# Where V is turned and split in a stick-breaking attention block: whole on TensorE before it is stored, or chunk by chunk after it is loaded

## The reference, cut to what matters

```python
z = einsum('bhqd,bhnkd->bhqnk', q_blk, k_pre) * scale
log_1m = where(valid, log_sigmoid(-z), 0.0)
within = einsum('bhqnk,kj->bhqnj', log_1m, suffix)
w = where(valid, exp(log_sigmoid(z) + within + later[..., None]), 0.0)
o = einsum('bhqnk,bhnkd->bhqd', w, v_pre)
```

## Time and profile before

| | |
|---|---|
| median of three runs | 2293.88 us |
| the profiled execution | 2293.96 us |
| its span, first to last instruction | 2292.2 us |
| TensorE busy | 2279.5 us, 99% |
| VectorE, ScalarE, GpSimd busy | 1444.4, 1060.2, 1224.3 us |
| granted TensorE clock | 0.999 of full speed |

### The profile page before, as it was taken

One profiled execution on the slowest core, in us unless ns is written; L12 is line 12 of the kernel. 1 busy time (PEld: TensorE's weight loads), 2 busy tenths in 40 slices (PEclk: granted clock), 3 DMA queues, 4 the chain that ended last, 5 costly groups with the idle time before them and its releaser, 6 DMA issues.

```text
span 2292.2 us, 29991 instructions
## 1 busy us (share of the span) xinstructions
PE 2279.5 (99%) x10824; PEld 1886.8 (82%) x10824; DVE 1444.4 (63%) x1658; ACT 1060.2 (46%) x1627; POOL 1224.3 (53%) x847
## 2 busy tenths in 40 slices
PE   9999999999999999999999999999999999999998
PEld 6888888888878888888888888888888778888887
DVE  7565542764496478568877777733854585486476
ACT  5555542343385255332576676632342583355220
POOL 1666643865456355435476566644863556456341
PEclk9999999999999999999999999999999999999999
DMA  6544422123334345373344543322133334354442
GB/s 234 187 159 158 139 83 97 55 83 129 113 104 133 134 124 148 105 284 138 108 159 139 165 156 124 125 92 78 56 120 124 92 103 134 130 156 132 152 161 83
DMA packets 114419, 297.84 MB, mean 130 GB/s; under 512 B 11232, under 2 KB 41056, under 8 KB 113248
## 3 DMA queue, kind: packets, MB, share of 16 engines
q1 hardware_dynamic: 112544, 290.68, 38.6%
q10 hardware_dynamic: 1728, 5.24, 0.7%
HBM read 216.19 MB, written 71.30 MB: 125 GB/s over the span
## 4 chain that ended last, share of the span: by engine, by line
PE 97%; DVE 1%; DMA 1%; issue 0%; DVEq 0%
PE J L823 21%; PE J L825 21%; PE J L824 21%; PE ZZ L995 8%; PE AO L995 8%; PE ZZ L825 2%; PE ZZ L824 2%; PE ZZ L823 2%; PE AO L825 2%; PE AO L824 2%; PE AO L823 2%; PE AO L949 1%; PE JX L949 1%; PE ZZ L1030 1%; PE JX L825 1%; PE JX L823 1%
## 5 line engine op out<-in xcount | busy, mean ns | idle before, releaser
L2341 POOL TENSOR_TENSOR WLS<-SR,WHS 128x512 fp32r<-128x512 f32 x264 | 414.3, 1588 | 110.1 <-ACT WHS L1161 102.5
L823 PE MATMUL J<-XBH,WHS 128*128 128x512 f32 x1152 | 452.3, 393 | 0.0
L825 PE MATMUL J<-XBH,WLS 128*128 128x512 f32 x1152 | 449.1, 390 | 0.0
L824 PE MATMUL J<-XBL,WHS 128*128 128x512 f32 x1152 | 448.9, 390 | 0.0
L823 PE MATMUL J<-XBH,WH 128*128 128x512 f32 x864 | 340.3, 394 | 0.4 <-DVE WL L1764 0.2
L825 PE MATMUL J<-XBH,WL 128*128 128x512 f32 x864 | 337.0, 390 | 0.0
L824 PE MATMUL J<-XBL,WH 128*128 128x512 f32 x864 | 336.8, 390 | 0.0
L825 PEld LDWEIGHTS J<-XBH,WLS 128*128 128x128 f32 x1152 | 216.2, 188 | 46.0
L824 PEld LDWEIGHTS J<-XBL,WHS 128*128 128x128 f32 x1152 | 216.4, 188 | 43.6 <-issue 0.2
L823 PEld LDWEIGHTS J<-XBH,WHS 128*128 128x128 f32 x1152 | 216.4, 188 | 43.5 <-issue 0.2
L2333 POOL TENSOR_TENSOR SR<-RAW 128x512 f32<-128x512 f32 x71 | 100.6, 1417 | 269.8 <-DMA RAW<-w 230.8
(11 more groups left out here) (305 smaller groups left out, 4753.3 us busy)
## 6 DMA issues: line engine op xcount, KB each, us to landing
RAW<-w SPq DMA_DIRECT2D x144, 512.0 KB, 3.7
pk_m<-MB SPq DMA_DIRECT2D x56, 512.0 KB, 5.0
MB<-pk_m SPq DMA_DIRECT2D x48, 512.0 KB, 3.9
KC<-pk_k SPq DMA_DIRECT2D x40, 512.0 KB, 5.4
VC<-pk_v SPq DMA_DIRECT2D x40, 512.0 KB, 4.4
BRAW<-w SPq DMA_DIRECT2D x64, 256.0 KB, 5.0
XRAW<-xt SPq DMA_DIRECT2D x8, 1024.0 KB, 12.6
pk_v<-STL SPq DMA_DIRECT2D x16, 512.0 KB, 5.0
```

Of the source, the lines that this page charges most:

```text
L823: nc.tensor.matmul(to, wh, xh, start=first, stop=True, skip_group_check=True)
L824: nc.tensor.matmul(to, wh, xl, start=False, stop=True, skip_group_check=True)
L825: return nc.tensor.matmul(to, wl, xh, start=False, stop=True, skip_group_check=True)
L2341: low = G_.tensor_tensor(WLS[:, k, :], SR[:, k, :], WHS[:, k, :].bitcast(F32), ALU.subtract)
```

## The change: what it does

V is turned by VectorE: `turn_values` transposes blocks of 32 by 32 (two instructions of 128x512 a head, behind piece 10) into the place of the keys, and one store of 512 KB keeps it, unsplit. TensorE's `turn` and its waits on `v_blk` are gone. `load_v` brings a chunk into a new tile VRAW, 256 KB, by four DMAs of 32 partitions each, in runs of 512 bytes; they finish the transposition. It waits until GpSimd has read the chunk before. ScalarE copies the chunk into VC as the hi part (`values_hi`) and GpSimd subtracts for the lo part (`values_lo`), once a chunk, 40 chunks, in the step whose number is 1 modulo 4, behind that step's sigmoids and weights; both read VRAW in runs of 32 elements. `values` waits for GpSimd's part.

To make room for VRAW, REST has three slots instead of four, used in turn by step number. A place shift of one element per round keeps the element that the next chunk's scan starts from. TURN is 2 instead of 3: TensorE turns the weights of a step one step earlier. The splits stay four steps behind (SPLIT). The tiles behind REST move by 64 bytes, and three waits of projection copies name the new semaphores (left out below, as one of the same kind is shown).

```diff
 LAST, QUARTER = 896, D // 4
-TURN, TAIL = 3, 5
+TURN, SPLIT, TAIL = 2, 4, 5
+
+SLOTS, SHIFTS = 3, 5
 LEAD = ((4, 4, 4, 4), (4, 2, 2, 2))
...
     return half * HEADS * NS[0] + h * NS[half]
+def rest_place(half, s):
+
+    c, k, j, a, diag, end = STEPS[half][s]
+    return SHIFTS - (s - (ENDS[half][c - 1] + 1 if c else 0)) // SLOTS + a
+
+
 def first_group(half, h):
...
         SHARE = [at(f"SHARE{i}", R + 28 + 2 * i, [C]) for i in range(2)]
-        REST = at("REST", R + 32, [BLOCKS, C + 2])
+        REST = at("REST", R + 32, [SLOTS, SHIFTS + C + 1])
+        VRAW = at("VRAW", R + 38.09375, [C])
...
         pk_k = nc.dram_tensor("pk_k", (HEADS, P, SEQ // C, 2, C), F32).ap()
-        pk_v = nc.dram_tensor("pk_v", (HEADS, P, SEQ // P, 2, P), F32).ap()
+        pk_v = nc.dram_tensor("pk_v", (HEADS, P, SEQ // P, P), F32).ap()
         pk_y = nc.dram_tensor("pk_y", (2, P, T), F32).ap()
...
             return ACC if c and h + 1 == HEADS else JX
+        def chunk_moved():
+
+            return VRAW[:].rearrange("p (i b r) -> p b i r", i=GROUPS, b=BLOCKS)
+
+        def chunk_part(part):
+
+            return VC[:, :, part, :].rearrange("p b (i r) -> p b i r", i=GROUPS)
+
         def as_moved(c):
...
                 hh = half * HEADS + h
-                for part, of in ((1, places(half, STL)[1]), (0, places(half, STL)[2])):
-                    sp.wait_ge(v_blk, 2 * hh + 2)
-                    sp.dma_start(pk_v[h, :, half * TB:(half + 1) * TB, part, :],
-                                 of[:].bitcast(F32).rearrange("p (b m) -> p b m", m=P)).then_inc(v_kept[part], 16)
+                sp.wait_ge(v_tr, NC * (hh + 1))
+                sp.dma_start(pk_v[h, :, half * TB:(half + 1) * TB, :],
+                             places(half, ST)[1][:].rearrange("p (b m) -> p b m", m=P)).then_inc(v_kept, 16)
             def load_k(half, h, i):
...
                 if i == 0:
-                    for kept in v_kept:
-                        sp.wait_ge(kept, 16 * (half * HEADS + h + 1))
-                    if h == 0:
-                        wait_if(sp, o_out[1], 16 * 3 * half)
-                wait_if(sp, pv_done, 2 * n)
-                sp.dma_start(VC[:].bitcast(F32), pk_v[h, :, BLOCKS * (k ^ 1):BLOCKS * (k ^ 1) + BLOCKS]).then_inc(v_in, 16)
+                    sp.wait_ge(v_kept, 16 * (half * HEADS + h + 1))
+                wait_if(sp, vc_lo, n)
+                for q in range(GROUPS):
+                    rows = pk_v[h, :, GROUPS * (k ^ 1) + q].rearrange("(i x) m -> x i m", i=GROUPS)
+                    to = VRAW[SQUARE * q:SQUARE * (q + 1)].rearrange("x (i m) -> x i m", i=GROUPS)
+                    sp.dma_start(to, rows).then_inc(v_in, 16)
             def piece(g, i):
...
                         load_v(half, h, 0)
-                    elif BLOCKS < s <= ns and s % BLOCKS == 0:
-                        load_v(half, h, s // BLOCKS - 1)
+                    elif BLOCKS < s < ns and s % BLOCKS == BLOCKS - 1:
+                        load_v(half, h, s // BLOCKS)
                     if BLOCKS <= s and s % BLOCKS == 0 and s + BLOCKS < ns:
...
                     wait_if(pe, ad_done, 4 * (g - 1) + 2)
-                    if 2 <= l <= 2 * HEADS and l % 2 == 0:
-                        pe.wait_ge(v_blk, 2 * (half * HEADS + l // 2))
                     if l == 0 and half:
...
                     mm.then_inc(pr_done, 1)
-                if l < 2 * HEADS and l % 2 and i in (10, 12):
-                    turn(g, 0 if i == 10 else 1)
-
-            def turn(g, part):
-
-                hh = g // PAIRS * HEADS + g % PAIRS // 2
-                v, c = places(g // PAIRS, ST)[2], J[(g + 1) % 2]
-                if part:
-                    pe.wait_ge(v_blk, 2 * hh + 1)
-                else:
-                    pe.wait_ge(ad_done, 4 * g + 2)
-                for j in range(4):
-                    mm = nc.tensor.transpose(c[:, j * P:(j + 1) * P], v[:, (4 * part + j) * P:(4 * part + j + 1) * P],
-                                             IDENT[:])
-                mm.then_inc(v_tr, 1)
             def pair(g, inside={}, first=0):
...
                 wait_if(pe, wt_lo, gs - 1)
-                n = C - a
+                n, first = C - a, rest_place(half, s)
                 for b in range(n // P):
-                    w = REST[:, j, n - P * (b + 1):n - P * b]
+                    w = REST[:, gs % SLOTS, first + n - P * (b + 1):first + n - P * b]
                     mm = nc.tensor.transpose(TB_[gs % 2][:, b * P:(b + 1) * P], w, IDENT[:])
...
                 pe.wait_ge(wt_lo, 2 * (gp + 1))
-                pe.wait_ge(v_in, 16 * (n + 1))
+                pe.wait_ge(vc_lo, n + 1)
                 blocks = j + 2 if diag else BLOCKS
...
                     if i % 2 == 0 and p:
-                        wait_if(act, v_kept[1], 16 * hh)
+                        wait_if(act, v_kept, 16 * hh)
                     elif i % 2 == 0 and i:
...
                     elif i % 2:
-                        wait_if(act, v_kept[0], 16 * hh)
+                        wait_if(act, v_tr, NC * hh)
                 elif kind == "merge" and i >= 2:
...
                     shared(g, 1, 0, 0, 6)
-                if g % PAIRS < 2 * HEADS and g % 2 and i in (10, 12):
-                    values_hi(g, 0 if i == 10 else 1)
-
-            def values_hi(g, part):
-
-                hh = g // PAIRS * HEADS + g % PAIRS // 2
-                act.wait_ge(v_tr, 2 * hh + part + 1)
-                nc.scalar.copy(places(g // PAIRS, STL)[2][:, part * C:(part + 1) * C], J[(g + 1) % 2][:]).then_inc(v_hi, 1)
+
+            def values_hi(half, h, i):
+
+                n = first_group(half, h) + i
+                act.wait_ge(v_in, 16 * GROUPS * (n + 1))
+                wait_if(act, pv_done, 2 * n)
+                if h == 0 and i == 0:
+                    wait_if(act, o_out[1], 16 * 3 * half)
+                nc.scalar.copy(chunk_part(0), chunk_moved()).then_inc(vc_hi, 1)
             def split_keys(g):
...
                 for s in range(ns + TAIL + 1):
-                    if 0 <= s - TURN - 1 < ns:
-                        turned_hi(half, h, s - TURN - 1)
+                    if 0 <= s - SPLIT < ns:
+                        turned_hi(half, h, s - SPLIT)
                     if s < ns:
                         shares(half, h, s)
+                    if TAIL <= s < ns + BLOCKS and s % BLOCKS == 1:
+                        values_hi(half, h, s // BLOCKS - 1)
                     if s == ns and h + 1 < HEADS:
...
                 V_.tensor_tensor(d, bank[:], d, ALU.add).then_inc(ad_done, 1)
-            def turned(g, part):
+            def turn_values(g):
                 hh = g // PAIRS * HEADS + g % PAIRS // 2
-                t = slice(part * C, (part + 1) * C)
-                dve.wait_ge(v_hi, 2 * hh + part + 1)
+                dve.wait_ge(ad_done, 4 * g + 2)
                 dve.wait_ge(k_kept, 32 * (hh + 1))
-                hi, lo = places(g // PAIRS, STL)[2], places(g // PAIRS, STL)[1]
-                V_.tensor_tensor(lo[:, t], J[(g + 1) % 2][:], hi[:, t].bitcast(F32),
-                                 ALU.subtract).then_inc(v_blk, 1)
+                _, to, v = places(g // PAIRS, ST)
+                for c in range(NC):
+                    t = slice(c * C, (c + 1) * C)
+                    V_.transpose(to[:, t].rearrange("p (q b x) -> p b q x", q=GROUPS, b=BLOCKS),
+                                 v[:, t].rearrange("p (b n) -> p b n", b=BLOCKS)).then_inc(v_tr, 1)
             def rest_of_first(g, parts=(0, 1)):
...
                     rest_of_sums(g + 1, False)
-                if l < 2 * HEADS and l % 2 and i in (10, 12):
-                    turned(g, 0 if i == 10 else 1)
+                if l < 2 * HEADS and l % 2 and i == 10:
+                    turn_values(g)
             def pair(g, after={}, first=0):
...
                 dve.wait_ge(share_done, gs + 1)
-                n, before = C - a, C - STEPS[half][s - BLOCKS][3]
+                n, before = C - a, rest_place(half, s - BLOCKS) + C - STEPS[half][s - BLOCKS][3]
                 if h == 0 and s < 2:
                     dve.wait_ge(ones_made, half + 1)
-                wait_if(dve, wt_done, gs - BLOCKS + 1)
-                V_.tensor_tensor_scan(REST[:, j, 0:n + 1], KEEP[:, gs % 2, 0:n + 1], ZB[gs % 2][:, 0:1].broadcast_to([P, n + 1]),
-                                      1.0 if diag else REST[:, j, before:before + 1], ALU.mult, ALU.bypass
+                wait_if(dve, wt_done, gs - SLOTS + 1)
+                first = rest_place(half, s)
+                V_.tensor_tensor_scan(REST[:, gs % SLOTS, first:first + n + 1], KEEP[:, gs % 2, 0:n + 1],
+                                      ZB[gs % 2][:, 0:1].broadcast_to([P, n + 1]),
+                                      1.0 if diag else REST[:, (gs - BLOCKS) % SLOTS, before:before + 1], ALU.mult, ALU.bypass
                                       ).then_inc(scan_done, 1)
...
                         piece(*pieces.pop(0))
```

(39 more changed lines are left out.)

## The result

The kernel after took **2304.43 us** (median of four runs, 2303.46 to 2306.39), the kernel before beside it 2294.08. The ratio is 1.0046, 95% interval 1.0029 to 1.0064: 10.4 us slower. Predicted were 2295.7 and a range up to 2301.5; it lies above the range. The profiled execution took 2303.46 us, with a span of 2301.5, at a clock of 0.999 of full speed, so the clock has no part in it.

What follows compares the result with a forecast made beforehand. The prediction took TensorE as the bound, busy 2279.5 of 2292.2 us. Gains of -9.0 plus 6.0 stalls, 1.0 refill and 3.8 GpSimd gave +1.8, so 2295.7 us, range 2286.5 to 2301.5.

Steps and rivals of the forecast that it cites:

- The stalls of TURN 2: TensorE's turn of the weights waits for VectorE's split to free its PSUM bank, in 29 places: +6.0 us.
- the refill: Each stall also refills TensorE's pipeline, 0.04 us in some 25 places: +1.0 us, from 0 to 2.
- GpSimd's part: GpSimd's `values_lo`, 1.30 us each, delays its multiplications, and ScalarE's copy delays VectorE: +3.8 us, between 0 and 10.
- Removed from TensorE: TensorE: 16 transpose bursts gone, -7.2 us; waits on `v_blk`, -1.0; wait for V's load, -0.8.
- the load's 0.8: TensorE's three waits for the load of V disappear if its new way is early: -0.8 us.
- VectorE's transposes at 0.62 us, nothing: VectorE: 16 transposes of 128x512 at 0.62 us replace 16 subtractions of 0.68 us, at no cost.
- 0.85 with 0.06 us from semaphore to matmul: Last head: the new turn's place is 0.79 us before its split ends, 0.85 with the 0.06 us release delay.
- the walk: Stalls of the 160 turns followed head by head with the shift carried along; nothing in three heads, 3.2 us at most.
- first rival: The stalls in the attention are mostly not there; with 2 us of stalls the time is 2287; chance 0.27.
- second rival: GpSimd bounds the attention steps because its split takes up to 2.33 us, not 1.30: 2302; chance 0.20.
- The load, cost taken 0: SyncE's four loads a chunk land within 4.6 us, upper bound 9, against 7.3 us of cover: 0.
- third rival: Loads of V land late; some 36 chunks each wait 0.2 us or more: 2303 or slower; chance 0.05.

Runs made afterwards that it cites:

- the short part: The changed kernel with GpSimd's lo part made for 32 of a chunk's 512 elements, except the first chunk of a half: 2302.12 us, ratio 1.0036.

## Why the prediction was wrong

The time is above the range because two steps failed. The stalls of TURN 2 were priced too low: +7.0 with the refill, measured +11.1. And the late load and the store of V were put at 0 and measured 4.0. The gains fell short by 2.1 (-9.0, measured -6.9), and GpSimd's part was too high by some 1.5 (+3.8, measured +2.3). Together these four make 8.7 us, and the forecast was 8.6 short (+1.8 for +10.4).

The measured parts, from separate kernels: no turn on TensorE -6.9, TURN 2 +11.1, GpSimd's part +2.3, store and load +4.0; sum +10.5, against +10.4 measured. Each part has an uncertainty of some 3 us, and GpSimd's leaves a place out, so that they add up to a tenth is luck. The signs and sizes of the first two are clear of noise; of the other two only that they cost something, by runs that hardly overlap and by waits in the traces.

- **Removed from TensorE, -9.0: -6.9.** The bursts were right (-7.2; measured 7.1). The waits on `v_blk` (-1.0) were hardly worth anything, and of the load's 0.8 the experiment tests only the 0.6 that went by itself: a middle head of the first half becomes 0.92 us shorter without the turn and 0.87 longer with a second one, so all else in it is 0.05 us.
- **VectorE's transposes at 0.62 us, nothing.** They take 684 ns in the median, and nobody waits for them. The rule of the Trainium skill ("VectorE: DVE Perf Modes", "Rules for kernel authors") gives a 128x128 transpose to TensorE. In this kernel, whose bound is TensorE, taking it away gained 6.9 us as long as the blocks stayed unassembled; the complete kernels, which assemble them and carry TURN 2 with it, gained nothing.
- **TURN 2, +6.0 and +1.0 for the refill: +11.1.** The mechanism was right and so were most places, the size was not. The step that failed is "0.85 with 0.06 us from semaphore to matmul". Behind VectorE's split it is 0.15 us; 0.06 is what the trace of the kernel after shows behind GpSimd. In 28 places that is 2.5 us of the 2.95 that were lacking in the walk (8.95 by starts). The walk also had nothing in the first three heads, where each has one late turn of 0.24 us and is 0.35 us longer. The refill was about right, 0.8 us for 1.0. With the 0.7 us of longer waits for the load that makes 10.5 of the 11.1 us; the rest is not traced. So the first rival ("the stalls are mostly not there", 0.27) got the largest chance that any rival had, and was the furthest off.
- **GpSimd's part, +3.8: +2.3, and somewhat more with the place left out.** The place given at step 5 of the second half's first head is there: the turn at 1163.64 comes 1.5 us late by starts, 0.9 more than the same turn with TURN 2 alone, predicted 1.2 more. The next two heads did not feel it, and in the last one its first eleven steps took 0.9 us more than with the short part, predicted 1.3. The **second rival** fell: the split took 1292 ns in the median and 1611 at most, never 2.33:

```profile
L2402 POOL TENSOR_TENSOR VC<-VRAW,VC x40: 1266/1292/1611, 94.1 to 1478.0; 128x512 fp32r<-128x512 f32 x40
```

The traces also answer what the prediction left open, what stands beside the long ones. Two of the 40 took over 1.31 us, 1.43 and 1.61, and they are the two that ran beside VectorE's line 1787, which reads two tiles of SBUF:

```profile
1372.81 2.02 DVE L1787 TENSOR_TENSOR STL<-ST,KHT 128x1024 fp32r<-128x1024 f32 x1
1374.36 1.61 POOL L2402 TENSOR_TENSOR VC<-VRAW,VC 128x512 fp32r<-128x512 f32 x1 [0.61 <-ACT VC L1277]
```

In the kernel before, 102 of the 264 splits of the earlier trace rows had no VectorE instruction beside them whose two source tensors are both in SBUF, and none of these took over 1.31 us; of the 162 others 108 took over 1.4, up to 2.33. So the rival's price exists, but its condition is rare where `values_lo` stands.

- **The load, cost taken 0: it and the store cost 4.0 us.** The step that failed is "needed four steps later ... if SyncE stands in front of a weight load at that moment, a step or so of this cover goes, not all". A weight load did stand in front in the two places that cost TensorE time, and no cover was left there: 0.7 and 1.2 us came back when the load went ahead of it. In three more the stores of keys stood in front, which the prediction did not have. The load was asked for at step 3 modulo 4 where it could go at step 2. In the last head its delay reached TensorE through ScalarE's copy, the split and the turn. The **third rival** (0.05) had the mechanism, though not at 36 chunks: five waits were enough. Its rows were about how long a DMA takes, when the question was when it is issued.
- **The store of V** was in the sum as "a store of 512 KB is saved". The prediction did not look at when it lands. It was 0.89 us late before; the change moved it no earlier although V is ready sooner, and ahead of the copy that reuses its place there was no slack: 1.8 us in that head, 2.4 in the medians, when undone alone.

## What to carry to other kernels

Software pipelining by a constant is paid at the tightest step, and a stall by a semaphore costs TensorE the lead of its weight load as well: read the time from release to matmul at a stalled place with the same releaser (here 0.15 us behind VectorE, 0.06 behind GpSimd). A stage that moves a step earlier moves all its parts: look for what each part waits for, the buffer that it writes too. For each DMA that is moved, read what stands ahead of it in its queue, and what reuses its source, before asking how long it takes. And split a bundle: here the part that gained 6.9 us came with three that cost some 17, and the constant that freed the buffer cost more than the buffer's use gained.

## What the runs showed of the hardware

- From the end of VectorE's split to the turn's matmul 0.15 us (0.12 to the weight load, 0.03 to the matmul) in 28 places of TURN 2 alone; from the end of GpSimd's multiplication 0.06 us in four places of the kernel after, the weight load starting with the matmul. An unhindered weight load leads its matmul by 0.23 us.
- A GpSimd split of 128x512 took at most 1.31 us where no VectorE instruction with two source tensors in SBUF ran beside it (102 in the kernel before, 36 in the kernel after on line 2402), and up to 2.33 us where one did.
- GpSimd's subtraction of 128x512 that reads one source in runs of 32 elements took 1292 ns in the median; the contiguous one took 1301.
- Four loads of 64 KB to 32 partitions landed 3.1 us after their issue in the median, 2.1 us when issued a step earlier; a load of 512 KB to 128 partitions took 4.4.
